# A bias added to the residual by GpSimd instead of by four two-row products on TensorE, in a two-block transformer kernel

## What is computed

```
    _, hs = lax.associative_scan(combine, (a, b_seq), axis=1)
    out = hs.astype(h.dtype) * y_br
    return jnp.einsum('bse,ed->bsd', out, w_o) + b_o
...
        h = h + mix
        h = h + sq_relu_mlp(rmsnorm(h, norm_mlp[layer]), mlp_w1[layer], mlp_w2[layer])
```

## Time and profile before

| | |
|---|---|
| median of 3 runs | 1010.04 us (1009.45 to 1010.71) |
| the profiled execution's own time | 1010.41 us |
| its span in the profile | 1008.6 us |
| PE, share of the span busy | 99% |
| DVE | 68% |
| ACT | 55% |
| POOL | 3%, 37 instructions |
| HBM read | 182.81 MB |

### The profile page before, as it was taken

One profiled execution on the slowest core, in us unless ns is written; L12 is line 12 of the kernel. 1 busy time (PEld: TensorE's weight loads), 2 busy tenths in 40 slices (PEclk: granted clock), 3 DMA queues, 4 the chain that ended last, 5 costly groups with the idle time before them and its releaser, 6 DMA issues.

```text
span 1008.6 us, 14152 instructions
## 1 busy us (share of the span) xinstructions
PE 1001.3 (99%) x5620; PEld 857.4 (85%) x5620; DVE 683.2 (68%) x925; ACT 556.0 (55%) x804; POOL 34.5 (3%) x37
## 2 busy tenths in 40 slices
PE   9999999999999999999999999999999999999997
PEld 7988788888889988888888888888888788888886
DVE  5777676666667887666566767565668867666564
ACT  6678654444446866444444655545467664645453
POOL 1000010000002300000000100000010010000000
PEclk9999999999999999999999999999999999999999
DMA  9943385665563545755655566665625465665621
GB/s 334 307 157 126 126 273 176 201 210 173 172 204 112 181 167 188 243 175 172 207 206 167 176 216 195 211 201 178 200 87 147 136 199 170 224 209 167 209 84 43
DMA packets 124559, 184.80 MB, mean 183 GB/s; under 512 B 3162, under 2 KB 103182, under 8 KB 124366
## 3 DMA queue, kind: packets, MB, share of 16 engines
q1 hardware_dynamic: 122304, 176.70, 53.3%
q0 software_dynamic: 1728, 6.60, 1.8%
q10 hardware_dynamic: 462, 0.60, 0.2%
HBM read 182.81 MB, written 1.07 MB: 182 GB/s over the span
## 4 chain that ended last, share of the span: by engine, by line
PE 96%; DVE 3%; ACT 1%; issue 0%; POOL 0%; DVEq 0%; POOLq 0%
PE bank L1532 36%; PE bank L1509 28%; PE bank L1511 14%; PE bank L1495 3%; PE bank L1497 3%; PE bank L1498 3%; PE bank L1707 1%; PE bank L1558 1%; DVE w_lo L829 1%; PE bank L1683 1%; PE bank L1653 1%; PE bank L1667 1%; DVE work L1006 0%; PE bank L1852 0%; PE bank L1853 0%; PE bank L1854 0%
## 5 line engine op out<-in xcount | busy, mean ns | idle before, releaser
L829 DVE TENSOR_TENSOR w_lo<-raw,w_hi 128x2048 fp32r<-128x2048 f32 x164 | 374.0, 2290 | 130.6 <-ACT w_hi L426 130.5
L1509 PE MATMUL bank<-xT,w_hi 128*128 128x512 f32 x1216 | 431.3, 398 | 0.0
L1511 PE MATMUL bank<-xT,w_lo 128*128 128x256 f32 x1216 | 341.0, 280 | 0.0
L426 ACT ACTIVATE w_hi<-raw 128x2048 fp32r<-128x2048 f32 x164 | 311.7, 1908 | 35.6 <-PE bank L1532 32.7
L1509 PEld LDWEIGHTS bank<-xT,w_hi 128*128 128x128 f32 x1216 | 228.4, 188 | 55.7 <-issue 0.3
L1511 PEld LDWEIGHTS bank<-xT,w_lo 128*128 128x128 f32 x1216 | 229.5, 189 | 1.9
L1532 PE MATMUL bank<-w_hi,z_hi 128*128 128x512 f32 x472 | 153.5, 393 | 0.1
L1532 PE MATMUL bank<-w_lo,z_hi 128*128 128x512 f32 x472 | 152.3, 391 | 0.0
L1532 PE MATMUL bank<-w_hi,z_lo 128*128 128x512 f32 x472 | 151.7, 390 | 0.0
L470 ACT ACTIVATE work<-bank 128x256 f32<-128x256 f32 x152 | 49.8, 380 | 178.5 <-PE bank L1511 178.5
L904 DVE TENSOR_TENSOR work<-bank,work 128x256 f32<-128x256 f32 x152 | 57.1, 418 | 73.9 <-ACT work L470 73.9
(11 more groups left out here) (213 smaller groups left out, 771.4 us busy)
## 6 DMA issues: line engine op xcount, KB each, us to landing
raw<-in_w SPq DMA_DIRECT2D x64, 1024.0 KB, 5.3
raw<-in_f_gate SPq DMA_DIRECT2D x22, 1024.0 KB, 5.4
raw<-in_f_up SPq DMA_DIRECT2D x22, 1024.0 KB, 5.9
raw<-in_f_down SPq DMA_DIRECT2D x22, 1024.0 KB, 5.0
raw<-in_w_in SPq DMA_DIRECT2D x11, 1024.0 KB, 5.5
raw<-in_w_qkv SPq DMA_DIRECT2D x9, 1024.0 KB, 9.0
raw<-in_w_o SPq DMA_DIRECT2D x4, 1024.0 KB, 5.0
raw<-in_rec_w_o SPq DMA_DIRECT2D x4, 1024.0 KB, 5.8
```

Source lines behind the costliest of these rows:

```text
L426: e.activation(*by_channel(n, w_hi[n % RING], raw[n % RAW]), ACT.Copy).then_inc(hi_done, 1)
L829: e.tensor_tensor(low_, here, high, ALU.subtract).then_inc(lo_done, 1)
L1509: e.matmul(bank[i], whi[:, k, cut], xT[:, k, :, :].rearrange("p b s -> p (b s)"), start=(k == 0), stop=False, skip_group_check=True)
L1511: last = e.matmul(bank[i][:, 0:S], wlo[:, k, cut], xT_hi[:, k, :], start=False, stop=(k == KB - 1), skip_group_check=True)
```

## The change

The four two-row products are taken out, with ACT's and DVE's preparation of their operands and the tiles `both` and `firsts`. b_o is loaded straight into a float32 tile of its own, by the same DMA at the same place in POOL's queue. POOL, behind the last of its squares, adds this tile to each half of h (128 x 1024 each) in place. DVE waits for both adds before it begins the adds of the closing of this stage. The first output piece now opens the four banks.

```diff
-    b_o = sb("b_o", [P, D], F32R)
-    both = sb("both", [P, P], F32R)
-    firsts = sb("firsts", [P, 2])
+    b_o = sb("b_o", [P, D])
...
-        def bias_hi():
-            e.wait_ge(in_b_o, 16)
-            e.activation(b_o, bo_raw, ACT.Copy).then_inc(bo_hi, 1)
-            e.activation(both, ones[:, 0:P], ACT.Copy).then_inc(bo_hi, 1)
-
         turn(M0, N_WO + 3 + LOOK)
-        feed_forward(FM0, bias_hi)
+        feed_forward(FM0)
...
-        def bias_split():
-
-            e.tensor_tensor(firsts, ident[:, 0:2], ident[:, 32:34], ALU.add).then_inc(bo_rest, 1)
-            for i in (2, 3):
-                e.wait_ge(bo_rest, i - 1)
-                e.tensor_tensor(firsts, firsts, ident[:, 32 * i:32 * i + 2], ALU.add).then_inc(bo_rest, 1)
-            e.wait_ge(bo_hi, 1)
-            e.tensor_tensor(bo_low, bo_raw, r32(b_o), ALU.subtract).then_inc(bo_rest, 1)
-            e.wait_ge(bo_rest, 4)
-            e.tensor_scalar(bo_low, bo_low, firsts[:, 1:2], None, ALU.mult).then_inc(bo_rest, 1)
-            e.wait_ge(bo_rest, 5)
-            e.scalar_tensor_tensor(out=b_o, in0=r32(b_o), scalar=firsts[:, 0:1], in1=bo_low, op0=ALU.mult,
-                                   op1=ALU.add).then_inc(bo_done, 1)
-
         turn(M0, FM0.n0)
-        feed_forward(FM0, bias_split)
+        feed_forward(FM0)
...
         lo(FM1.n0)
 
+        e.wait_ge(bo_done, T)
         turn(M1, FM1.n0, 1)
...
-        e.dma_start(bo_raw, row_bcast(A["b_o"], D)).then_inc(in_b_o, 16)
+        e.dma_start(b_o, row_bcast(A["b_o"], D)).then_inc(in_b_o, 16)
...
         for p in range(4):
             squares(p)
+
+        e.wait_ge(in_b_o, 16)
+        e.wait_ge(turned, KB * L1 + KB)
+        for t in range(T):
+            e.tensor_tensor(h[:, t, :], h[:, t, :], b_o, ALU.add).then_inc(bo_done, 1)
         e.wait_ge(var_done, M1 + 1)
         e.dma_start(nf, row_bcast(A["norm_final"], D)).then_inc(in_norm_final, 16)
...
-        e.wait_ge(bo_done, 1)
-        e.wait_ge(bo_hi, 2)
         e.wait_ge(ig_done, KB)
-        for t in range(T):
-            for half in range(2):
-                r = slice(32 * (2 * t + half), 32 * (2 * t + half) + 2)
-                e.matmul(acc[t][half], both[r, :], b_o[r, half * HALF:(half + 1) * HALF], start=True, stop=False,
-                         skip_group_check=True)
         for i in range(2):
             e.wait_ge(mix_lo, 4 + i + 1)
-            d_piece(N_RO + i, from_z(i))
+            d_piece(N_RO + i, from_z(i), first=(i == 0))
```

More of the change, by code:

```diff
@@ L207, in build @@
         "a_done", "sq_done", "m_done", "mult_done", "b_done", "hs_done", "y_done", "o_done"))
-    bo_hi, bo_rest, bo_done = sem("bo_hi"), sem("bo_rest"), sem("bo_done")
+    bo_done = sem("bo_done")
     mix_left, pc_closed, pc_left, pool_d, d_left, v_turned, v2_done = (sem(n) for n in (
@@ L300, in rec_home @@
         return blocks(xT_hi, p), blocks(xT_lo, p)
-    bo_raw, bo_low = at(24, D), at(28, D)
     nf = at(8, D)
@@ L490, in normed_squares, with feed_forward @@
                 e.activation(at(16 + 4 * t, D), h[:, t, :], ACT.Square, accum_out=ssq2[:, t:t + 1]).then_inc(hn_ss, 1)
-        def feed_forward(f, beside=None):
+        def feed_forward(f):
             if f.nu == 2:
@@ L507, in feed_forward @@
                 n = f.ups(p)
-                if beside and p == 6:
-                    beside()
                 if n + LOOK < TOTAL:
@@ L979, in feed_forward @@
                 n = f.ups(p)
-                if beside and p == 7:
-                    beside()
                 if n + LOOK < TOTAL:
```

## The result

The changed kernel takes 1015.83 us (median of 5, 1014.93 to 1016.65) against 1010.04 us before (1009.35 to 1010.71): a ratio of 1.0057, 95% interval 1.0046 to 1.0068. It is slower by 5.8 us, where 4.3 had been forecast; 1015.8 lies inside the range, the sign is as forecast, and the distance is mostly a case that the prediction had as a rival.

A forecast was written before the change was run, and what follows sets the result against it. PE, busy 99% of the span, bounds the kernel. DVE late by 4.9 us makes PE start piece 56 4.3 us later, the 0.5 us gain already included: 1010.04 + 4.3 = 1014.3 us, range 1012.7 to 1017.2.

The forecast's parts named there:

- The removed parts: Bias preparation on DVE and ACT worth 0; four products on PE before output piece 56 worth 0.5 us.
- GpSimd and VectorE exclude each other: From 349.85 us, DVE instructions reading two SBUF tensors stand while POOL adds; DVE late by 4.9 us.
- The price of an add: Each 128 x 1024 add on POOL takes 2.45 us, 4.9 for both, with 4.2 and 5.2 as ends.
- The stall: PE waits some 4.7 us for DVE's mixed_lo(0) before output piece 56, starting it at 361.77 instead of 357.47: +4.3 us.
- the signs that were to show it: PE wait of about 4.7 us released by DVE's L1240, two 2.45 us adds, lengthened DVE instructions, equal 11.11 us periods.
- second wait: After piece 56 PE and DVE are late by nearly the same amount, so no second stall through closing.
- the new wait of VectorE: DVE's wait for both adds before the closing's adds costs 0, since POOL is done by 356.
- The narrow margin at closing: PE needs mixed_lo(3) for closing at 376.79; DVE's side has it at 376.55.
- Pushed back: Rival: DVE always gets in first, POOL's adds start after y_pair(2) at 356.69; +3.5, 1013.5 us; chance 0.13.
- hidden: Rival: the adds run beside DVE undisturbed, only the products' 0.5 us is left, 1009.5 us; chance 0.07.
- The clock: Rival: the stall before piece 56 lowers PE's clock, 2.1 us more, 1016.4, or about 3 us, 1017.3; chance 0.27.
- The price taken from the start of the kernel: Twelve 512-column products at the start took 4.89 us, the next twelve 2.75; difference 2.1 us.

The follow-up runs named there:

- the run without adds: Changed kernel without GpSimd's two adds and without DVE's wait for them, the recurrence's bias left out: 1009.11 us, ratio 0.9994 to the kernel before.
- The memsets: Changed kernel with five GpSimd memsets of 128x1024 into an unused tile in place of the two adds, bias left out: 1009.40 us, ratio 0.9998.
- the kernel before with adds: Kernel before, products and preparation kept, plus two GpSimd adds of 128x1024 behind its squares into an unused tile: 1016.02 us, ratio 1.0066.
- the kernel with 9 products: Changed kernel with 9 extra float32 products of 256 columns on PE where it would wait before output piece 56: 1014.16 us, ratio 1.0039.
- the two comparisons: Changed kernel against the kernel before, measured twice: 1015.83 us, ratio 1.0057, and again with a second profile 1015.28 us, ratio 1.0056.
- the four quarters: Changed kernel with the same additions as four 128x512 GpSimd adds at places where VectorE waits or works from PSUM: 1009.20 us, ratio 0.9994.

## Why the prediction was right, and where it was off

**The removed parts.** Preparation worth 0, products 0.5 us: borne out as far as times reach. In the timelines the distance shrinks by 0.53 us in the run without adds, but by 0.34 us when only the products go; the other 0.19 us was put down to them too.

**GpSimd and VectorE exclude each other.** Right, and now on the instructions that had not been seen: inflow and the scans stand beside an add as L1220 did beside a square. The memsets, 4.5 us of them, add that an instruction of GpSimd that only writes does not do it. This is what the Trainium skill (SBUF — State Buffer, Who interferes with whom) says, with its clause on instructions that only write, and these runs agree.

**The price of an add.** Taken as 2.45 us, it was 2.28 to 2.29. I went near the bx row doubled; a quarter of 128 x 512 took 1.27 to 1.30 again, so the part paid once is nearly 0.3 us, more than I allowed. The 4.5 us that were estimated from the Trainium skill's page (GPSIMD Engine Reference) were nearer: measured 4.57 for both.

**The stall.** PE's wait was put at some 4.7 us and was 4.22. The steps are right and the term for the adds was too large: VectorE late by 4.4, not 4.9. Of the signs that were to show it, one did not: the changed kernel's profile names no releaser for the wait; that of the kernel before with adds names VectorE's mixed_lo. The stall alone makes the +4.0 of the kernel with 9 products. No second wait appeared, and the new wait of VectorE cost nothing: at the first add of the closing it stood 2.50 us for PE, with GpSimd long done. The narrow margin at closing, 0.24 us, held in the profiles with the clock at 1.00 too (with 9 extra products, 84 products in 19.34 us without a gap).

**Pushed back, or hidden.** Neither happened. Where both engines are queued up, the one that waits gets its turn as the other ends an instruction, so they alternated (mults, add, mults, add, inflow), and GpSimd was never starved.

**The clock: the step that failed.** I made the lower clock a rival with 0.27, because the trace of before had no fall from the higher level in it. It belonged in the sum. In both profiles of the changed kernel the granted clock falls to 0.50, 1.1 us before the wait ends in one and 0.1 us after it in the other, with 2.7 and 1.6 us more for the same products. The price taken from the start of the kernel, 2.1 us, lies between them, which is in part luck. The prediction has only "small work with waits" in front of the slow products there; the trace has 32 small products in a row, six more, and one wait of 0.3 us:

```profile
0.99 3.60 PE L1691 MATMUL bank<-zeros 128*128 128x128 bf16 x32 [0.99 <-POOL zeros L1427]
```

With 4.0 for the wait, 1.8 and 1.5 us are left for the clock of the 5.8 and 5.5 us that the two comparisons give. So the forecast of 1014.3 was off by a term left out (+1.5 to +1.8) and one too large (-0.3 on the sum), and 1015.8 came inside the range because the range had been drawn to take in the clock. The missing row was no evidence against. That idleness lowers the clock is what the Trainium skill (TensorE: Matmul & The Clock Gate, What's actually happening) states, and these traces agree.

## What to carry to other kernels

An idle GpSimd is not free help for a full VectorE: here each add on it took its own length, 2.28 us, from VectorE's instructions with two SBUF inputs. So look for stretches where VectorE waits or reads PSUM, and cut the work to fit them, as the four quarters did at no cost. Behind a stall of PE of some 2 us or more reckon with slow products too, 1.5 to 2.7 us here where the clock fell, and with more scatter between executions than the kernel without the stall has. A cost that a trace cannot show because nothing in it ever stalled belongs in the forecast by its likelihood, not by its absence.

## What the runs showed of the hardware that was not expected

A wait of PE of 2.0 us lowered the granted clock in one profile and left it in the other, with the waits equal to 0.01 us; one of 1.9 us near the start of the run with memsets lowered it; waits of 3.7 us (one profile), 4.2 us (two) and 8.4 us (one) lowered it each time, and in the two profiles in which PE was kept at work but for 0.2 and 0.3 us it stayed. The time lost at the lower level does not grow with the wait: 84 products lost 2.6 us behind 3.7 us, 2.7 and 1.6 behind 4.2, 1.5 behind 8.4, where much of the low stretch passed while PE was still idle. The fall came at anything from 3.8 us before PE started again to about 0.8 us after. What decides the moment of the fall was not tried.

GpSimd's add of 128 x 1024 in float32 takes 2.28 us and of 128 x 512 1.29 us, the square of 128 x 512, with one tensor as both inputs, 1.04 us.
